# Mixer attention and gated linear branch issued inside the projection, in two buffer groups; modulation loads split over both mixers

## The reference, cut to what matters

```
mod = silu(c) @ w_ada[l] + b_ada[l]            # 6 vectors of 1024: shift, scale, gate for mixer and experts
h = rms_norm(x) * (1 + scale_m) + shift_m
proj = h @ w_in[l]                             # 3088 columns: q, k, v (512 each), g_q, g_k (256), g_v, g_r (512), g_lr (16)
# A: 8 heads of 64 columns, key before query only
z = rms(q) . rms(k) / 8
w = exp(log_sigmoid(z) + suffix sum of -softplus(z));  out_a = w @ v
# B: 4 heads, chunks of 64 tokens
log_g = log_sigmoid(g_lr @ w_gk2 + b_gk) / 16; b = cumsum(log_g) in a chunk
o = intra(q e^b, k e^-b, v) + (q e^b) @ state; out_b = rms(o) * silu(g_r)
x = x + gate_m * (concat(out_a, out_b) @ w_out[l])
```

## Time and profile before

| | us |
|---|---|
| median of 3 runs | 3682.7 |
| lowest, highest | 3671.77, 3684.79 |
| the profiled execution's own time | 3683.26 |
| span of its trace | 3681.6 |
| mean granted TensorE clock | 0.933 |
| PE busy / VectorE busy / ScalarE busy | 3272.6 / 2207.3 / 1499.4 |
| mixer 0: start to x ready (L502 of the next stage) | 0 to 338.8 |
| of it from h ready (first L1521) | 91.0 to 338.8 |
| mixer 1 from h ready | 779.0 to 995.2 |

### The profile page before, as it was taken

How to read it: one execution, slowest core, us unless ns; L and a number is a source line. 1 busy time by engine, 2 the same in 40 slices (tenths; PEclk the granted TensorE clock), 3 DMA queues, 4 the chain that set the end, 5 groups by cost and what they waited for, 6 DMA issues and landing times.

```text
span 3681.6 us, 50054 instructions
## 1 busy us (share of the span) xinstructions
PE 3272.6 (89%) x17360; PEld 2808.8 (76%) x17360; DVE 2207.3 (60%) x4324; ACT 1499.4 (41%) x2375; POOL 161.9 (4%) x297
## 2 busy tenths in 40 slices
PE   1947899986689999789989999997879989999997
PEld 1736788764578887668878999996758878999996
DVE  4463677621267773629986666664628996666564
ACT  0131566613146662411853444442421773444442
POOL 2120000000000000005000000000004100000000
PEclk9967899988689999899999999998889999999998
DMA  5762688622057884124136555554214236555552
GB/s 198 257 210 89 242 300 300 255 89 74 25 208 284 293 301 153 46 83 143 64 126 195 184 189 184 188 188 143 79 48 138 87 98 195 186 189 184 188 187 92
DMA packets 166716, 614.78 MB, mean 167 GB/s; under 512 B 18704, under 2 KB 18736, under 8 KB 165536
## 3 DMA queue, kind: packets, MB, share of 16 engines
q1 hardware_dynamic: 151200, 551.62, 44.4%
q0 software_dynamic: 15360, 61.16, 4.8%
HBM read 611.66 MB, written 1.05 MB: 166 GB/s over the span
## 4 chain that ended last, share of the span: by engine, by line
PE 61%; DVE 10%; ACT 2%; DVEq 2%; issue 1%; DMA 0%; ACTq 0%
PE PS L1465 14%; PE PS L1466 14%; PE PS L1467 14%; PE PS L1490 6%; PE PS L1906 4%; PE PS L1927 2%; PE PS L1926 1%; DVE arena L1336 1%; DVE arena L1337 1%; DVE arena L1343 1%; PE PS L1740 1%; PE PS L1812 1%; DVE arena L1367 1%; PE PS L1736 1%; PE PS L1801 0%
## 5 line engine op out<-in xcount | busy, mean ns | idle before, releaser
L886 DVE TENSOR_TENSOR w_lo<-arena,w_hi 128x1024 fp32r<-128x1024 f32 x448 | 530.1, 1219 | 1.9 <-ACT w_hi L514 1.9
L514 ACT ACTIVATE w_hi<-arena 128x1024 fp32r<-128x1024 f32 x448 | 452.1, 1054 | 122.2 <-DMA arena<-in_v_t 87.4
L1467 PE MATMUL PS<-x_hi,w_lo 128*128 128x256 f32 x1536 | 434.7, 283 | 0.0
L1466 PE MATMUL PS<-x_lo,w_hi 128*128 128x256 f32 x1536 | 434.6, 283 | 0.0
L1465 PE MATMUL PS<-x_hi,w_hi 128*128 128x256 f32 x1536 | 433.7, 282 | 0.0
L1465 PE MATMUL PS<-w_hi,pw_hi 128*128 128x512 f32 x1024 | 404.1, 395 | 19.1 <-DVE w_lo L886 19.1
L1466 PE MATMUL PS<-w_lo,pw_hi 128*128 128x512 f32 x1024 | 402.7, 393 | 0.0
L1467 PE MATMUL PS<-w_hi,pw_lo 128*128 128x512 f32 x1024 | 400.4, 391 | 0.0
L808 ACT ACTIVATE arena<-PS 128x256 f32<-128x256 f32 x192 | 73.9, 385 | 636.4 <-PE PS L1467 636.4
L1440 DVE TENSOR_TENSOR arena<-arena 128x256 f32<-128x256 f32 x192 | 81.8, 426 | 392.3 <-ACT arena L808 392.3
L1107 DVE TENSOR_TENSOR gu_lo<-raw,gu_hi 128x1024 fp32r<-128x1024 f32 x256 | 297.4, 1221 | 30.2 <-ACT gu_hi L592 30.0
(11 more groups left out here) (418 smaller groups left out, 5851.0 us busy)
## 6 DMA issues: line engine op xcount, KB each, us to landing
raw<-in_w_gu SPq DMA_DIRECT2D x256, 512.0 KB, 5.4
arena<-in_u_t SPq DMA_DIRECT2D x256, 512.0 KB, 4.4
arena<-in_v_t SPq DMA_DIRECT2D x256, 512.0 KB, 3.6
arena<-in_w SPq DMA_DIRECT2D x152, 512.0 KB, 3.5
raw<-in_w_down SPq DMA_DIRECT2D x128, 512.0 KB, 5.4
arena<-in_w_ada POOLq DMA_DIRECT2D x96, 512.0 KB, 5.0
arena<-in_tab POOLq DMA_DIRECT2D x2, 1664.0 KB, 14.4
arena<-in_x POOLq DMA_DIRECT2D x2, 1632.0 KB, 9.7
```

The source lines that it names most:

```text
L514: A(w_hi[:, m % RING], ring[:, m % RING], ACT.Copy).then_inc(S["hi_done"], 1)
L886: V.tensor_tensor(w_lo[:, m % RING], ring[:, m % RING], w_hi[:, m % RING].bitcast(F32), ALU.subtract)\
L1466: mm(dst, w[0], m[1], start=False, stop=False)
L1467: return mm(dst, w[1], m[0], start=False, stop=stop)
```

## The change

- The `w_ada` tiles are taken in a new order, 16 for the columns m = 0 and 1, then 32 for m = 2 to 5, for both layers (`ada_step`). Layer 0: 16 before the first norm, 32 between VectorE's steps in mixer 0. Layer 1: 16 during the output projection of mixer 0, and 32 between the steps of mixer 1, which had none. The accumulator has one place for both layers and is no longer cleared (the first row of tiles is a plain multiply).
- The softplus attention has a buffer pair for each group of 4 heads (z0, e0 and z1, e1; results are written in place) and banks of its own for each group (4 to 6, and 0 to 2).
- Sums of squares, scores of group 0 and branch B's transposes stand between the pairs of the projection; scores of group 1 and the suffix sums of group 0 stand before the token-major products, and the rest between and behind these. g_v is now taken before v (`W1_ORDER`).
- PE's column sums for m = 2 to 5 stand behind the values and before `w_out`, in both mixers; those for layer 1's m = 0, 1 at the end of mixer 0.

PE's part of the diff (the other engines' parts follow the same order):

```diff
                 for j in pairs(n0, p0, 8, h):
                     if j == 0:
                         pe.wait_ge(S["glr_ev"], l + 1)
...
-                pe.wait_ge(S["gkz_ev"], 2 * (l + 1))
-                token_major(n0 + 16, 4)
-                if l == 0:
-                    ada_cols(1, 2)
-                    pe.wait_ge(S["ada_col"], 2)
-                token_major(n0 + 20, 6)
-                pe.wait_ge(S["qk_sq"], l + 1)
...
+                    if j == 4:
+                        pe.wait_ge(S["gkz_ev"], 2 * (l + 1))
+                        pe.wait_ge(S["qk_sq"], l + 1)
+                        for i in range(4):
+                            last = mm(PS[:, 4 + i, :], cc("headblk"), M["sq"][:, 2 * i:2 * i + 2], start=True, stop=True)
+                        last.then_inc(S["qk_ss"], 1)
+                    if j == 6:
+                        pe.wait_ge(S["qkn"], l + 1)
+                        scores(0)
+                        pe.wait_ge(S["gl_prod"], l + 1)
...
+                pe.wait_ge(S["pair_evac"], p0 + 7)
+                scores(1)
+                suffix(0)
+                pe.wait_ge(S["pair_evac"], p0 + 8)
+                pe.wait_ge(S["kend_ev"], l + 1)
+                token_major(n0 + 16, 0, 4)
+                pe.wait_ge(S["arg_ok"], 2 * l + 1)
...
+                suffix(1)
+                pe.wait_ge(S["gv_ev"], l + 1)
+                pe.wait_ge(S["sc_ok"], l + 1)
...
+                token_major(n0 + 20, 0, 2)
                 pe.wait_ge(S["states"], l + 1)
...
+                token_major(n0 + 20, 2, 4)
                 pe.wait_ge(S["o_sq"], l + 1)
...
+                pe.wait_ge(S["sbv_ev"], l + 1)
+                heads(0)
+                heads(1)
+                ada_cols(l, 2, NMOD, 7)
+                pe.wait_ge(S["outa_ev"], 2 * (l + 1))
                 pe.wait_ge(S["mixb_ok"], l + 1)
                 for _ in pairs(n0 + W1_IN, p0 + 8, 4, M["mixT"]):
                     pass
```

VectorE's modulation steps in the new order (`ada_part(n)` takes the next n of the 32 tiles, 4 + 14 + 3 + 3 + 2 + 2 + 4):

```diff
+                ada_part(4)
 
                 dve.wait_ge(S["gl_ln"], l + 1)
...
                 V.memset(G["st"], 0.0)
-                if l == 0:
-                    ada1(0, 8)
+                ada_part(14)
 
                 dve.wait_ge(S["qk_rs"], l + 1)
...
+                masked(0)
+                ada_part(3)
+                log_fail(0)
+                masked(1)
+                ada_part(2)
+                argument(0)
+                log_fail(1)
+                ada_part(2)
...
+                argument(1)
...
+                ada_part(4)
                 dve.wait_ge(S["o_rs"], l + 1)
...
                     last.then_inc(S["pair_evac"], 1)
-                if l == 0 and ("mix", 1) in plan:
-                    dve.wait_ge(S["ada_ps"], 3)
-                    ada_mod(1, 0, 2)
+                    if l == 0:
+                        ada(1, 4 * j, 4 * j + 4)
+                if l == 0:
+                    ada_mod(1, 0, 2, 6)
```

More of the change, by code:

```diff
@@ L414, in _, with ada @@
         def _(pool):
[L415 to L434, removed]
+            def ada(n0, n1):
+                for n in range(n0, n1):
+                    l, k, m = ada_step(n)
+                    if n >= 3:
+                        pool.wait_ge(S["ada_used"], n - 2)
+                    wk = a["w_ada"][l].rearrange("(k p) (m n) -> k m p n", p=P, n=D)
+                    pool.dma_start(ADA["ring"][:, n % 3], wk[k, m]).then_inc(ada_ready[n % 3], 16)
             def peer_ids(l):
@@ new lines, in weights @@
+                def weights(g):
+                    act.wait_ge(S["arg_ok"], 2 * l + g + 1)
+                    A(M[f"z{g}"], M[f"z{g}"], ACT.Exp).then_inc(S["w_ok"], 1)
+                evac(0)
+                act.wait_ge(S["gkz_mm"], l + 1)
+                for q in range(2):
+                    A(G["gy"][:, q], PS[:, 5, T * q:T * q + T], ACT.Identity, bias=c1(l, "b_gk", q, 1)).then_inc(S["gkz_ev"], 1)
+                act.drain()
+                b0 = G["b0"].rearrange("p (q c) t -> p q (c t)", q=2)
@@ L1493, in pairs, with token_major @@
                     yield j
[L1495 to L1497 removed]
+            def token_major(n0, i0, i1):
+                for i in range(i0, i1):
                     s = n0 + i
@@ L1522, in mix, with scores, near, far @@
                 last.then_inc(S["glr_mm"], 1)
+                q_, k_, v_ = M["qkn"][:, 0:4], M["qkn"][:, 4:8], M["sbv"]
+                def scores(g):
+                    b = 4 - 4 * g
+                    def near(par):
+                        for i in (par, par + 2):
+                            o, t = SBD * par, 2 * g + i // 2
+                            last = mm(PS[:, b + par, T * (i // 2):T * (i // 2) + T], k_[o:o + SBD, t, 0:P], q_[o:o + SBD, t, :], start=True, stop=True)
+                        return last
+                    def far(par):
+                        for i in (par, par + 2):
+                            o, t = SBD * par, 2 * g + i // 2
+                            last = mm(PS[:, b + 2, P * (2 * par + i // 2):P * (2 * par + i // 2) + P], k_[o:o + SBD, t, P:T], q_[o:o + SBD, t, P:T],
+                                      start=True, stop=True)
+                        return last
+                    far(0).then_inc(S["z_mm"], 1)
+                    near(1)
+                    near(0)
+                    pe.wait_ge(S["z_mm"], 2 * (2 * l + g) + 1)
+                    far(1).then_inc(S["z_mm"], 1)
@@ L1610, in mix @@
                     pass
-                if l == 0 and ("mix", 1) in plan:
-                    pe.wait_ge(S["ada_acc"], 3)
-                    for j in range(NMOD * KT):
-                        last = mm(PS[:, 6, j:j + 1], ADA1["acc"][:, j // KT, P * (j % KT):P * (j % KT) + P], ones[:, 0:1], start=True, stop=True)
-                    last.then_inc(S["ada_ps"], 1)
+                if l == 0:
+                    ada_cols(1, 0, 2, 6)
             def scatter_first(l):
```

294 lines of the change are left out of this document (132 added, 162 removed).

## The result

The changed kernel takes 3553.55 us (median of four runs, 3544.96 to 3558.94) against 3682.13 for the kernel before (3671.77 to 3684.79): a ratio of 0.9653, 95% interval 0.9633 to 0.9673. Forecast were 3569 and a range of 3540 to 3600.

The account below looks back on a forecast made before the run. PE, busy 89% of the span, was taken as the bound, so time comes off only its idle, lower-clock or unavoidable-chain stretches. -23.6 - 39.7 - 51.4 = -114.7 us from 3683.3 gave 3569 us, range 3540 to 3600.

Parts of the forecast that it names:

- The start of mixer 0: Before mixer 0's first product: 16 tiles instead of 24, fewer column sums, no clear; -23.6 us, h ready at 67.4.
- PE's work in mixer 1: PE's busy time in mixer 1 with no wait: 166.0 us, including 10.6 for new column sums; whole mixer 176.5, -39.7.
- so I take 31: Mixer 1's thin short products: 39 us at present pace, 25 at the upper clock level, taken as 31, so -8.
- The two waits: In each mixer PE waits for VectorE: 2.8 us before the first scores, 3.6 before the first suffix sums.
- The clock behind them: In each mixer, PE's lower clock after its two idle pieces costs 3 us in all.
- Mixer 0: From h ready to x: 196.4 us against 247.8, -51.4; 175.4 to the end of `w_out`.
- The tail: End of mixer 0: PE idles 13 us for layer 1's first 16 tiles, then column sums take 6.9 us.
- all is covered: Rival: in both mixers waits and clock loss vanish and short products run at full pace; 3540 us, chance 0.15.
- Late all the way: Rival: VectorE's queue runs 10 us late per mixer, adding a wait at group 1's suffix sums; 3590 to 3600, chance 0.16.
- no overlap: Rival: VectorE reaches the first mask so late that attention stands alone behind the projection; 3641 us, chance 0.04.
- slower: Rival: in the mixers GpSimd's tiles lose against SyncE's weights for DMA engines, blocking attention; 3729 us, chance 0.03.
- the one on DMA: Sign to look for: DMA above 300 GB/s in the projections of both mixers.

Follow-up runs that it names:

- The first experiment: Kernel before the change, with only layer 0's 48 tiles split into 16 ahead of the norm and 32 behind it: 3674.04 us against 3687.37.
- without cover: Changed kernel with all token-major products ahead of group 1's scores and the suffix sums, none between the steps of attention: 3602.17 us.
- The experiment without tiles: Changed kernel without the 32 tiles of layer 1's second part, their loads and steps in mixer 1; column sums still run on other data: 3540.32 us.
- the ring of 5: Changed kernel with 5 buffers instead of 3 for the landing modulation tiles: 3514.9 us.
- the combination: Changed kernel with 5 tile buffers, layer 1's first 16 tiles taken earlier in mixer 0, and the norm's sums ahead of the column sums: 3496.83 us, ratio 0.9507.
- the change's second run: Changed kernel measured once more, unaltered, on the same chip as the kernel with three further edits together: 3546.3 us, ratio 0.9642 to the kernel before.

## Why the prediction was right, point by point

- **The start of mixer 0**: -23.6 forecast, -23.7 measured, and part of the match is luck. The last tile was done 21.6 us earlier (46.5 instead of 68.0) where the text had 18.1 + 2, and the norm's sums behind the column sums took 6.5 instead of 5.2 us, which it had left alone. The first experiment, which keeps the clear, has its 16th tile at 48.1 and the norm's sums at 5.35, and comes out at 23.2.
- **PE's work in mixer 1**: it makes up most of the 12.2 us by which mixer 1 was shorter than forecast, and the term that was mis-sized is "so I take 31". The thin work took 24.6 us: scores 4.5, transposes 1.1, suffix sums 7.2, the other branch's products 6.6, its square sums 1.9, the heads 3.5 (neighbours overlap by a little). That is 6.4 less than taken and close to the 25 that the text had given for the upper level throughout. The reason named for staying above it, weight loads that set the pace of short products, fell: with and without cover those products take 4.4 and 8.7 us, close to the full factor of the clock. The column sums were 10.6 forecast, 8.8 in this trace and about 10.8 in most. `w_out` took 29.7 instead of 30.5. With 0.75 less of waits and 1.7 less of clock behind them (pair 7 lost 1.3 of the 3; what the scores lost is within the 24.6) that is 6.4 + 1.8 + 0.8 + 0.75 + 1.7 = 11.5 of the 12.2.
- **The two waits**: 2.8 and 3.6 forecast, 4.00 and 1.65 in mixer 1 and 2.43 and 4.97 in mixer 0: right in place and in the sum (6.4 against 5.7 and 7.4). The releaser was VectorE each time, but what made it late was not always a tile. In mixer 1 the log stood for 0.77 us behind ScalarE's third pass of softplus (773.02, above), which the text had ruled out: softplus was done 76.2 us behind h, as forecast (76.1), but the six tiles were done at 75.5, sooner than the 77.6 forecast. In mixer 0 the log followed straight behind a modulation step. Taking the tiles away removed the first and left 0.69 of the second.
- **The clock behind them**: 3 us forecast. Pair 7 lost 1.3 in mixer 1, and the window 145 to 152 of mixer 0 read 0.54, in which the first suffix sums took 6.6 us instead of 3.6. The experiment without tiles puts it at 3.0 in mixer 1 (1.2 of pair 7, 1.8 of the scores and what follows them). The Trainium skill (TensorE: Matmul & The Clock Gate, "HAM oscillation — how this bites in real kernels") describes a kernel in which every wait between bursts of matmuls puts PE back to half rate. Here the waits of 4.00 and 4.97 did, and those of 1.65 and 2.43 did not.
- **Mixer 0**: to the end of `w_out` 175.4 forecast, about 167.8 measured (the end of the last pair, at 235.1), so 7.6 less, against 12.1 less in mixer 1 (163.3). The same mis-sized term stands in both; mixer 0 gave back 3.1 us in its first suffix sums at half rate, 1.75 in longer waits and 1.3 in column sums (10.17 instead of 8.83), less some 2.8 us that mixer 1 lost behind its first wait. These make 3.4 of the 4.5 between the two. The tail was right: 13 us of idle forecast and 13.77 measured, then 6.99 for 6.9.
- **Rivals**: *all is covered* (3540) is what the ring of 5 does and more; the changed kernel lies between it and the forecast, with the waits present and the thin work at full pace. In that rival I had tied the two together, and they are separate; its price also counts "some 5 of the 6 us left in the thin work" once, though each of two mixers has it. *Late all the way*, *no overlap* and *slower* did not occur; tiles came on average (126.9 - 94.6)/14 = 2.3 us apart behind the sum of mixer 0.
- **The signs**: the one on DMA missed. Above 300 GB/s in both projections was forecast, and mixer 0 had 254 from 67 to 129 at a DMA share of 0.72, mixer 1 had 256 from 696 to 760 at 0.73. The DMA engines had room beside the pairs; with five places the same stretch of mixer 1 (669 to 733) had 279 at 0.76.

## What to carry to other kernels

Where a thin chain of small matmuls moves beside dense work, price it at its full-clock pace. Here gaps of waiting cost their length and, in half-rate work around them, three fifths as much again (5 and 3 us, the tiles) to as much again (15 and 14 us, no cover). Loads that one engine consumes while another waits for it come at (landing time + step) / places, until the step or the DMA engines are slower: at the start, 4.7 us to land plus 1.28 us of step over three places make 2.0 us a tile, and 2.12 was measured; over five, 5.6 plus 1.28 make 1.38, and 1.46 was measured. And a piece of work moved off one path reappears where its data is next waited for: look there before you count the gain.

## What the runs showed of the hardware that was not expected

- One-column products (32 records) took 6.99 us behind an idle stretch and 4.33 or 3.63 straight behind `w_out`, at a granted clock of 0.82 and 1.00. 64 of them behind the heads took 8.8 to 11.6 us, at a granted clock of 0.82 down to 0.61 while PE was busy throughout; the heads just ahead of them ran at 1.00 in each of the six traces looked at.
- At the start of the program the clock column can't be read. In the changed kernel it says 1.00 from 46.7 to 53.6, where 32 one-column records took 6.96 us, as long as the 6.99 they took from 248.9 on at a reading of 0.50.
- Whether PE falls to half rate behind a gap isn't set by the gap alone. Scores behind an idle of 2.89 us began at full rate (0.37 us) and fell to half within some 1 us (pair 7 behind them took 7.65 instead of 7.07), and behind 3.60 us they began at half (0.58); suffix sums behind 2.96 us took 2.07 in one mixer and behind 3.10 they took 1.12 in the next, in one and the same execution. What else decides it was not tried.
- More tiles in flight moved more: at the start (12 to 48) a tile took 4.7 us to land with three places and 5.6 with five, yet the rate of the stretch from 13 to 37 rose from 264 GB/s at a DMA share of 0.80 to 371 at 0.99, and the combination had 376 at 1.00.

The rows for the second point are these, of the change's second run, timeline of PE: scores and suffix sums of mixer 0, then of mixer 1.

```profile
128.20 0.37 PE L1533 MATMUL PS<-arena 64*128 64x128 f32 x1 [2.89 <-DVE arena L912]
143.38 2.07 PE L1546 MATMUL PS<-arena,cst 128*128 128x512 f32 x2 [2.96 <-DVE arena L934]
...
757.30 0.58 PE L1533 MATMUL PS<-arena 64*128 64x128 f32 x1 [3.60 <-DVE arena L912]
772.48 1.12 PE L1546 MATMUL PS<-arena,cst 128*128 128x512 f32 x2 [3.10 <-DVE arena L934]
```
